# Two activation buffers start 16 bytes further into longer rooms, in a float32r transformer kernel

## The reference

```
def swiglu_ffn(x, w_gu, w_down):
    gate, up = jnp.split(x @ w_gu, 2, axis=-1)
    return (jax.nn.silu(gate) * up) @ w_down
...
    for layer in range(DEPTH):
        x = x + 0.5 * swiglu_ffn(rms_norm(x, ffn1_norm[layer]), ffn1_w_gu[layer], ffn1_w_down[layer])
        h = rms_norm(x, mix_norm[layer])
...
        x = x + 0.5 * swiglu_ffn(rms_norm(x, ffn2_norm[layer]), ffn2_w_gu[layer], ffn2_w_down[layer])
```

## Time and profile before

| | |
|---|---|
| median of three runs | 2693.83 us |
| lowest and highest | 2691.82 and 2696.59 us |
| the profiled execution's own time | 2694.12 us |
| its span, first to last instruction | 2692.0 us |
| TensorE matmul busy | 2613.1 us, 97% |
| VectorE busy | 1920.5 us, 71% |
| ScalarE busy | 1502.9 us, 56% |
| DMA | mean 166 GB/s |

### The profile page before, as it was taken

The page is one execution under the profiler, slowest core; times in us unless marked ns, Lnnn a source line. Parts: engine busy times, 40 slices in busy tenths (PEclk is TensorE's granted clock), DMA queues, the critical chain, the costliest instruction groups (busy, mean ns, idle before and its releaser), DMA issues.

```text
span 2692.0 us, 51716 instructions
## 1 busy us (share of the span) xinstructions
PE 2613.1 (97%) x18604; PEld 2410.1 (90%) x18604; DVE 1920.5 (71%) x3131; ACT 1502.9 (56%) x2579; POOL 201.6 (7%) x280
## 2 busy tenths in 40 slices
PE   8999799999999999999999999999999999999998
PEld 7998699999998899999998998989989999988997
DVE  7777676778777576777777667777787776676876
ACT  6556556556555656556555555655565555555554
POOL 0001001000000201000000160000000005300000
PEclk9999899999999999999999999999999999999999
DMA  7554244655554344555654543545545545335553
GB/s 261 202 189 135 87 134 156 225 202 183 186 187 157 102 158 136 188 186 169 204 187 142 179 157 103 165 154 185 186 154 187 187 143 171 126 118 165 172 187 109
DMA packets 122821, 445.80 MB, mean 166 GB/s; under 512 B 13688, under 2 KB 14712, under 8 KB 122688
## 3 DMA queue, kind: packets, MB, share of 16 engines
q1 hardware_dynamic: 120816, 436.79, 49.0%
q0 software_dynamic: 1872, 7.17, 0.7%
HBM read 442.86 MB, written 1.05 MB: 165 GB/s over the span
## 4 chain that ended last, share of the span: by engine, by line
PE 92%; DVE 5%; ACT 2%; issue 1%; DMA 0%; SPq 0%; ACTq 0%; DVEq 0%
PE bank L457 91%; DVE w_lo L1471 1%; PE bank L808 1%; DVE rt L1699 1%; DVE z L1537 1%; ACT w_hi L1037 0%; DVE rt L1493 0%; DVE x L1530 0%; DVE a L1498 0%; ACT score L1271 0%; DMA x<-in_x_dram 0%; DVE rstd_x L1490 0%; DMA raw<-in_stream_dram 0%; ACT L1245 0%; DVE z L1643 0%
## 5 line engine op out<-in xcount | busy, mean ns | idle before, releaser
L457 PE MATMUL bank<-a,w_hi 128*128 128x256 f32 (+1 forms) x5360 | 1342.3, 329 | 38.5 <-DVE a L1498 38.0
L1471 DVE TENSOR_TENSOR w_lo<-raw,w_hi 128x1024 fp32r<-128x1024 f32 x829 | 1016.7, 1230 | 278.3 <-ACT w_hi L1037 277.1
L457 PE MATMUL bank<-a,w_lo 128*128 128x256 f32 x3736 | 1013.2, 282 | 0.0
L457 PEld LDWEIGHTS bank<-a,w_hi 128*128 128x128 f32 x5360 | 897.4, 190 | 126.2 <-issue 45.7
L1037 ACT CAST w_hi<-raw 128x1024 fp32r<-128x1024 f32 x829 | 858.0, 1046 | 42.6 <-DMA raw<-in_stream_dram 35.4
L457 PE MATMUL bank<-b,w_hi 128*128 128x256 f32 (+1 forms) x4096 | 859.5, 301 | 3.6 <-DVE b L1498 2.6
L457 PEld LDWEIGHTS bank<-a,w_lo 128*128 128x128 f32 x3736 | 709.2, 190 | 16.8
L457 PEld LDWEIGHTS bank<-b,w_hi 128*128 128x128 f32 x4096 | 656.9, 188 | 40.6 <-issue 3.5
L457 PE MATMUL bank<-b,w_lo 128*128 128x256 f32 x2400 | 658.6, 280 | 0.0
L457 PEld LDWEIGHTS bank<-b,w_lo 128*128 128x128 f32 x2400 | 450.4, 188 | 5.6
L1084 ACT COPY pt<-bank 128x256 f32<-128x256 f32 x176 | 65.5, 372 | 219.1 <-PE bank L457 219.1
(11 more groups left out here) (185 smaller groups left out, 2130.7 us busy)
## 6 DMA issues: line engine op xcount, KB each, us to landing
raw<-in_stream_dram SPq DMA_DIRECT2D x829, 512.0 KB, 3.3
z<-in_biasc_dram POOLq DMA_DIRECT2D x6, 512.0 KB, 4.5
z<-in_biasa_dram POOLq DMA_DIRECT2D x3, 512.0 KB, 4.4
x<-in_x_dram SPq DMA_DIRECT2D x2, 512.0 KB, 8.0
v<-in_mem_dram POOLq DMA_DIRECT2D x2, 512.0 KB, 6.3
out_dram<-x SPq DMA_DIRECT2D x8, 128.0 KB, 1.9
con<-in_con_dram POOLq DMA_DIRECT2D x1, 912.0 KB, 6.6
vec<-in_vec_dram POOLq DMA_DIRECT2D x1, 417.0 KB, 5.6
```

Source lines behind the costliest of these rows:

```text
L457: return nc.tensor.matmul(out, lhsT, rhs, start=start, stop=stop, skip_group_check=shared)
L1471: return nc.vector.tensor_tensor(out, a, hi.bitcast(F32), ALU.subtract)
```

## The change

`a` and `b` become tensors of 4096 + 32 elements on each partition, 128 bytes longer than before. The buffer that the kernel uses is a view that starts 4 elements, 16 bytes, into that room. Both buffers therefore start at remainder 48 modulo 128 instead of 32. `b` moves by another 128 bytes, and everything behind it by 256 bytes, which leaves every other remainder modulo 128 as it was.

```diff
-        a_two, b_two = sb("a", [P, C, 2, T], F32R), sb("b", [P, C, 2, T], F32R)
+        ROOM, A_AT, B_AT = 32, 4, 4
+        a_room, b_room = sb("a", [P, C * 2 * T + ROOM], F32R), sb("b", [P, C * 2 * T + ROOM], F32R)
+        a_two, b_two = (room[:, at:at + C * 2 * T].rearrange("p (c s t) -> p c s t", s=2, t=T)
+                        for room, at in ((a_room, A_AT), (b_room, B_AT)))
```

## The result

The changed kernel takes 2712.41 us (2710.35 to 2714.61, four runs) against 2695.21 for the kernel before in the same runs: a ratio of 1.0065, 95% interval 1.0048 to 1.0083. It is 17 us slower. The profiled execution has a span of 2711.2 us against 2692.0, 19.2 more.

A forecast was written before the change was run, and what follows sets the result against it. The prediction took TensorE's products and the distance between their starts as the bound. Each moved address (streamed buffers, v_half's loads, writes) was valued at zero, so the forecast stayed at 2694 us, range 2640 to 2770.

The forecast's parts named there:

- What bounds the kernel: TensorE, busy 2613.1 of 2692.0 us: time is the number of products times the distance between their starts.
- The range: Whole kernel: 2640 to 2770 us, said to hold about 0.83.
- the upper bound: About 17,100 products, v_half's included, each paying 4.4 ns more: 75 us slower, 2769.
- The likeliest case: Whole kernel: no change, 2694 us, own range 2689 to 2699, chance 0.35.
- the first kind of instruction: The 15,592 TensorE products that stream a or b, their start going from 32 to 48 modulo 128; value taken zero.
- both rhythms: TensorE triples of 256-column products: a fast rhythm of 0.340 us and a slow one of 0.353.
- The faster rival: New offset lets more TensorE stretches fall into the fast rhythm: up to 79 us gained, 2615; chance 0.31.
- The split read: Line 457 products on a or b need one more fetch off 32-byte pieces: up to 75 us slower; chance 0.16.
- The slower rival by rhythm: Gate, up and down tiles settle in a worse rhythm: 0 to 75 us, a third giving 2719; chance 0.18.
- The write side: ScalarE and VectorE writes of high and low parts: 4 us if the uncovered writes slowed ten per cent; taken as zero.
- The rule on lines: SBUF cachelines are 16 bytes, so a 16-byte shift leaves every operand on as many lines: time stays 2694.
- The rule on ports: TensorE's moving operand and weight load have a read port each and wouldn't meet: shift does nothing, 2694.

The follow-up runs named there:

- e6: Kernel before with both buffers moved 128 bytes and all behind them 256, offset 64 to the weights: 2672.05 us, ratio 0.9916.
- e1: Changed kernel with its longer rooms kept but both buffers at the first byte, without the 16 bytes: 2684.36 us, ratio 0.9961 to the kernel before.
- e9: The 16 bytes of the change put on top of e6, both buffers at offset 48: 2712.11 us, ratio 1.0068 to the kernel before.
- e4: Changed kernel with a and b 32 bytes into their rooms instead of 16: 2711.21 us, ratio 1.006 to the kernel before.
- e10: Kernel before with a, b, w_hi and w_lo all starting 16 bytes off a multiple of 32, offset 64: 2672.01 us, ratio 0.991.
- e8: Kernel before with both buffers 16 bytes into rooms 256 bytes longer, all other remainders modulo 256 kept: 2713.48 us, ratio 1.0068.
- e2: Changed kernel with w_hi and w_lo 16 bytes further too, w_lo moving 128 bytes more than w_hi: 2688.53 us, ratio 0.9975 to the kernel before.
- e3: Changed kernel with buffers back at their rooms' first byte and w_hi, w_lo moved to remainder 80: 2710.25 us, ratio 1.0056 to the kernel before.
- e5: Kernel before with b and all behind it moved 256 bytes, a left in place: 2696.25 us, ratio 1.0001.

## Why the prediction was right or wrong

**What bounds the kernel** held: all of the 19 us is in TensorE's products, none on another engine. **The range** held: 2712 lies in 2640 to 2770, and the price stayed far under the 75 us of the upper bound.

**The likeliest case did not come.** The step that failed is the value taken for the first kind of instruction, "The value that I take is zero". It rested on two reasons. The first was that both rhythms exist at one set of addresses, "so an address doesn't choose between them by itself". The observation was true and the conclusion wrong: at a given offset a stretch can enter either rhythm, but the offset settles which rhythms there are and how often each is met. At 64 the down tiles run at 2.73 us; at 192 at 2.82 or 2.83; and at the change's offsets, down tiles at 48 run at 2.86 and mixer triples at 176 at 0.360, rhythms that the earlier trace rows don't have. Counting stretches of four triples that stream `a` shows the choice: before, 36 of 293 go at 0.340 to 0.343 us a triple and 196 at 0.352 to 0.355; in e6, 172 of 295 and 56; in the change none goes at 0.340. What the prediction put at nothing thus measured 17 us for the change, and 28 for its 16 bytes alone (e1 to the change). It also took the offset modulo 128, 64 going to 48; the number that counts was 192, going to 176 for a and 48 for b. The second reason was that the streams sweep all remainders, so that a shift changes where a collision falls and not how many there are. e9 measures 40 us for 16 bytes; whatever it is that collides, its count or its price does change.

**The faster rival** had its mechanism right: an offset can let more stretches fall into the fast rhythm. The argument against it ("the offset isn't what forbids it") was wrong, but 64 minus 16 bytes was not the offset that does it. e6 shows the gain that it spoke of: 23 us, against the bound of 79. The bound was too wide since gate and up tiles didn't go along. In e6 they still take 5.63 us, while down takes 2.73; its timeline:

```profile
1304.32 0.40 PE L460 MATMUL bank<-b,w_hi 128*128 128x256 f32 x2
...
1307.05 0.39 PE L460 MATMUL bank<-a,w_hi 128*128 128x512 f32 x1
...
1312.68 0.40 PE L460 MATMUL bank<-b,w_hi 128*128 128x256 f32 x2
```

A step of 8.36 us, where the bound had 8.16.

**The split read** foresaw a slower kernel for a reason that isn't there: e4 is slow on multiples of 32, e10 fast off them. It had also said that v_half would suffer least. In the change the mean distance between v_half's products grew from 115.2 to 118.2 ns, 2.6%, and that between the 256-column products that stream `a` from 117.3 to 119.1, 1.6% (distances over 200 ns, which hold a wait, left out of both). So v_half lost more.

**The slower rival by rhythm** is what happened, with 17 us where a third of its price gave 25. I had given it 0.18. Its picture of a mirror of the fast rhythm was roughly right for size: triples went 0.007 over the slow rhythm in the mixers, half of the 0.013 that I had taken.

**The write side** at zero was right: 424 and 552 ns.

**The rule on lines**, from the Trainium skill, page "SBUF — State Buffer", section "Specifications (TRN2)", gave no change for a shift of 16 bytes, since each operand stays on as many whole lines. The runs show 18, 28 and 40 us for such shifts (e8, e1 to the change, e9), while a shift of all four operands by 144 bytes shows none (e6 to e10). Whatever the size of a line, counting the lines of one operand is not enough. **The rule on ports**, from the Trainium skill, page "TensorE: Matmul & The Clock Gate", section "Step-by-step: what each phase is for", has the two reads pass each other freely; e8 and e10 contradict that in its effect, since with the buffers at one remainder 41 us hang on where the weights lie. The prediction also set 2.5 ns for each product against the 11 measured; by the page's section "Back-to-back issue gap" in the Trainium skill that figure is the gap of products alone, not of a stream with weight loads in between, so the two were never like for like.

**What stays open** is how the two reads get in each other's way. Measured are the offsets 64 (2672), 96 and 192 (2695), 128 (2709), 48 and 176 (2712 and 2713), with 160 for a and 32 for b 2711 (down tiles of 2.88 and 2.84 us). I see no simple rule in this order. No other offset was tried, and one offset for w_hi and another for w_lo only in e2 and e3. The eight networks are quickest in e2, 1416.6 us against 1420.0 in e6, so 2672 need not be the best that there is. That a step of 256 bytes changes nothing is shown for `a` alone: by e5 at offset 192, and by e10 beside e6 at 64, where the weights lie 256 bytes further from `a`.

## What to carry to other kernels

Where TensorE is the bound and each product comes with its own weight load, the distance in SBUF between the streamed and the loaded tensor is a setting worth 1.5% here (2672 to 2713), for 256 unused bytes on each partition. Hold it fixed modulo 256 when anything ahead in memory changes size, or a harmless edit will bring a gain or a loss that isn't its own: the longer rooms alone gave 11 us. Read it from the distance between the starts of neighbouring products, since the mean duration of a product shows it badly (282 ns for the products of `a` with w_lo, before and in the change alike), and try a distance against the weights, not an alignment of one tensor.

## What the runs showed of the hardware

- Two tensors that TensorE reads at once, one streamed and one loaded, interact by their offset modulo 256 bytes (2672 us in e10, 2713 in e8, same buffer addresses modulo 256), also while no other engine and no DMA is at work. A triple of 256-column float32r products was seen to take 0.340 us (offset 64, and at times 192), 0.353 (192), 0.357 (48) and 0.360 (176).
- Starts off a multiple of 32 bytes cost nothing in themselves that the total shows: 2672.01 us with all four tensors off, 2672.05 with all on.
- The kernels with remainders equal modulo 128 are not equal: 2695, 2684, 2689 and 2672 us for the four combinations of a and b moved by 128 bytes.
- The best distance differs by arrangement. From offset 192 to 64 the down tile gained 0.09 us, and the gate and up tiles of a step together lost 0.02. At 96 the gate and up tiles are quickest (2.785 us each, 2.822 at 64) and the tiles outside the networks slow.
- The gains are 11 us for b alone, 7 for a alone and 23 for both. The 5 us over their sum are within what the intervals leave open.
